# Half-array attention products in alternating pairs, in the mixing stage of a two-layer trunk

## The reference

```python
# branch A (dsa_attention), per query block of 128 tokens, 8 heads of 64, latents of 128
q_lat = jnp.einsum('bshd,rhd->bshr', q, w_uk)                       # Q
dots = jax.nn.relu(jnp.einsum('bqhd,bkd->bqhk', iq_b, ik) * idx_scale)
score = jnp.einsum('bqh,bqhk->bqk', iw_b * w_scale, dots)           # index scores
_, idx = lax.top_k(score, k_sel)                                    # 128 keys: the picks
logits = jnp.einsum('bqhr,bqkr->bqhk', ql_b, c_sel) * scale + bias  # A
p = jax.nn.softmax(logits, axis=-1)
o_lat = jnp.einsum('bqhk,bqkr->bqhr', p, c_sel)
return jnp.einsum('bqhr,rhd->bqhd', o_lat, w_uv)                    # U

# branch C (mem_attention), 4 heads of 64, 256 memory tokens
logits = jnp.einsum('bshd,bmhd->bhsm', q, k) * C_HEAD_DIM ** -0.5   # C
p = jax.nn.softmax(logits, axis=-1)
return jnp.einsum('bhsm,bmhd->bshd', p, v)                          # V
```

## Time and profile before

| what | value |
|---|---|
| median of 3 runs | 2313.9 us (2313.88 to 2318.39) |
| the profiled execution | 2316.2 us |
| its span, first to last instruction | 2314.4 us |
| mean granted TensorE clock | 0.996 |
| PE products; PE weight loads | 2259.5; 1837.9 us busy |
| DVE; ACT; POOL | 1250.9; 560.4; 1407.6 us busy |
| HBM | 90 GB/s over the span |

### The profile page before, as it was taken

One profiled execution on the slowest core, in us unless ns is written; L12 is line 12 of the kernel. 1 busy time (PEld: TensorE's weight loads), 2 busy tenths in 40 slices (PEclk: granted clock), 3 DMA queues, 4 the chain that ended last, 5 costly groups with the idle time before them and its releaser, 6 DMA issues.

```text
span 2314.4 us, 31805 instructions
## 1 busy us (share of the span) xinstructions
PE 2259.5 (98%) x10328; PEld 1837.9 (79%) x10328; DVE 1250.9 (54%) x1756; ACT 560.4 (24%) x1038; POOL 1407.6 (61%) x868
## 2 busy tenths in 40 slices
PE   7999999999999999999999999999999999999997
PEld 5888887777877788888888888877777878888885
DVE  5551554578766655145355335637787566540554
ACT  3120111443454211001121111214444532110111
POOL 4766768534445667667667666774444466666664
PEclk9999999999999999999999999999999999999998
DMA  6243223211212222322323332232112132223222
GB/s 166 93 136 104 98 79 121 83 55 55 69 60 81 93 91 91 100 100 86 105 92 126 107 105 96 80 115 73 56 60 69 46 100 91 100 82 109 99 78 77
DMA packets 67523, 209.79 MB, mean 91 GB/s; under 512 B 7369, under 2 KB 10601, under 8 KB 67177
## 3 DMA queue, kind: packets, MB, share of 16 engines
q1 hardware_dynamic: 63600, 202.84, 27.0%
q10 hardware_dynamic: 3832, 5.77, 1.1%
HBM read 204.91 MB, written 3.67 MB: 90 GB/s over the span
## 4 chain that ended last, share of the span: by engine, by line
PE 90%; DVE 7%; issue 1%; ACT 1%; DMA 0%; DVEq 0%; ACTq 0%
PE bank L521 28%; PE bank L523 27%; PE bank L522 27%; PE obank L741 1%; PE sbank L693 1%; PE tbank L714 1%; DVE u1L L1434 1%; DVE picks L1234 1%; DVE picks L1257 1%; DVE tb L1448 1%; PE sbank L688 1%; PE obank L728 1%; DVE top L1232 1%; PE sbank L675 1%; PE sbank L698 1%
## 5 line engine op out<-in xcount | busy, mean ns | idle before, releaser
L475 POOL TENSOR_TENSOR wL<-raw,wH 128x1024 fp32r<-128x1024 f32 (+3 forms) x432 | 952.6, 2205 | 36.1
L472 POOL TENSOR_SCALAR wH<-raw 128x1024 fp32r<-128x1024 f32 (+3 forms) x432 | 455.1, 1053 | 847.6 <-PE bank L523 832.5
L521 PE MATMUL bank<-u0H,wH 128*128 128x512 f32 x1408 | 552.7, 393 | 8.2 <-POOL wL L475 4.3
L523 PE MATMUL bank<-u0L,wH 128*128 128x512 f32 x1408 | 549.8, 390 | 0.0
L522 PE MATMUL bank<-u0H,wL 128*128 128x512 f32 x1408 | 549.7, 390 | 0.0
L521 PEld LDWEIGHTS bank<-u0H,wH 128*128 128x128 f32 x1408 | 265.2, 188 | 68.2 <-issue 9.0
L522 PEld LDWEIGHTS bank<-u0H,wL 128*128 128x128 f32 x1408 | 265.5, 189 | 55.5 <-issue 1.0
L523 PEld LDWEIGHTS bank<-u0L,wH 128*128 128x128 f32 x1408 | 265.4, 189 | 55.5
L521 PE MATMUL bank<-u1H,wH 128*128 128x512 f32 x704 | 295.6, 420 | 7.3 <-DVE u1L L1434 3.0
L521 PE MATMUL bank<-hidH,wH 128*128 128x512 f32 x704 | 275.1, 391 | 0.8 <-DVE hidL L1137 0.8
L523 PE MATMUL bank<-u1L,wH 128*128 128x512 f32 x704 | 275.1, 391 | 0.0
(11 more groups left out here) (175 smaller groups left out, 2400.1 us busy)
## 6 DMA issues: line engine op xcount, KB each, us to landing
raw<-in_wA SPq DMA_DIRECT2D x176, 512.0 KB, 3.3
raw<-in_wM SPq DMA_DIRECT2D x96, 512.0 KB, 3.3
raw<-in_wB SPq DMA_DIRECT2D x64, 384.0 KB, 3.0
raw<-in_wB SPq DMA_DIRECT2D x64, 320.0 KB, 2.9
raw<-in_wR SPq DMA_DIRECT2D x32, 256.0 KB, 2.6
h<-in_xT ACTq DMA_DIRECT2D x4, 512.0 KB, 7.0
mem<-in_memT SPq DMA_DIRECT2D x2, 1024.0 KB, 7.3
near_bias<-bias_rows ACTq DMA_DIRECT2D x2, 1024.0 KB, 6.8
```

The source lines that it names most:

```text
L472: pool.tensor_scalar(wH[:, w, 0:cols], raw[:, slot, 0:cols], 1.0, 0.0, ALU.mult, ALU.add).then_inc(rounded, 1)
L475: pool.tensor_tensor(wL[:, w, 0:cols], raw[:, slot, 0:cols], wH[:, w, 0:cols].bitcast(F32), ALU.subtract).then_inc(split_done, 1)
L521: pe.matmul(dst, a, hi[:, k, :], start=first and i == 0, stop=False)
L523: mm = pe.matmul(dst, a, lo[:, k, :], start=False, stop=last and i == len(tiles) - 1)
```

## The change

`attention_steps` has one Q step per block and one U step per block where there were two each, so eight steps fewer, in a new order. Each of these steps makes both halves. The C steps keep their number, but the logits of both halves are issued in the step of the first half, and the values of both in the later step, three behind the second half. Within a step the two halves alternate product by product: rows 0-63 and 64-127 for C and Q, each into a small bank of its own, columns 0-63 and 64-127 for V and U, into the two partition halves of one bank. PE waits for both small banks ahead of a C or Q pair. `olat` is two buffers. ACT copies two query halves in a Q step, and U's high and low part are one instruction each of 128 partitions. The numbers of products do not change.

C now stands at tile 0 of slots 6 to 13, scores beside tiles 6 and 7 of even slots and 1, 3, 5, 7 of odd ones, and "bc" slots 0 to 2 have no step. The last U stands behind tile 4 of slot 34, before slot 35.

```diff
 def attention_steps():
-    s = [("C", qb, hp) for qb in range(QB) for hp in range(2)]
-    s[4:4] = [("Q", 0, 0), ("Q", 0, 1)]
+    s = [("C", qb, hp) for qb in range(QB) for hp in range(2)] + [("Q", 0, 0)]
...
         if late:
-            a.insert(2, late)
-        at = a.index(("A", qb, 3))
+            a.insert(3, late)
         if qb + 1 < QB:
-            a.insert(at + 1, ("Q", qb + 1, 0))
-            a.append(("Q", qb + 1, 1))
-        at = a.index(("A", qb, 3))
-        a.insert(at + 4, ("U", qb, 0))
-        late = ("U", qb, 1)
+            a.append(("Q", qb + 1, 0))
         if qb == 0:
             a += [("B", 0, 0), ("B", 1, 0)]
+        late = ("U", qb, 0)
...
-SCORE_SLOTS = range(6, 12)
-FIRST_STEPS = 6
-ALONE = (6, 7, 8, 9, 11)
+FIRST_STEPS, FIRST_TWO = 6, 14
 AFTER = 8
-SCORES_BESIDE_TWO, SCORES_BESIDE_ONE = (1, 2, 6, 7), (2, 5, 6, 7)
+SCORES_BESIDE = ((6, 7), (1, 3, 5, 7))
+STEPLESS = (0, 1, 2)
...
+def picks_at(slot):
+    kind, i = slot
+    if kind == "bc":
+        return (0, int(i >= 3))
+    if i < 9:
+        return (0, 0)
+    if i < FIRST_TWO:
+        return (0, 2)
+    return (1, 2) if 16 <= i < 23 else (1, 1)
...
# PE, logits(i)
+                    if kind in "CQ":
+                        n, free = s_bank_free(("step", i + 1, 0) if kind == "C" else ("step", i, 1))
+                        if free:
+                            pe.wait_ge(*free)
+                        dst = [dst, sbank[n]]
                     if kind == "C":
...
-                        rows = slice(64 * b, 64 * b + 64)
                         for j in range(2):
-                            mm = pe.matmul(dst[:, j * M:(j + 1) * M], qc[rows, j, a * P:(a + 1) * P],
-                                           kc[rows, j, :], start=True, stop=True)
+                            for g in range(2):
+                                rows = slice(64 * g, 64 * g + 64)
+                                mm = pe.matmul(dst[g][:, j * M:(j + 1) * M], qc[rows, j, a * P:(a + 1) * P],
+                                               kc[rows, j, :], start=True, stop=True)
+                                if j == 1:
+                                    mm.then_inc(s_full, 1)
+                        return
...
                     elif kind == "U":
-                        pe.wait_ge(olat_ready, l * 8 + (2 * a + b + 1))
+                        pe.wait_ge(olat_ready, l * 8 + (2 * a + 2))
                         for j in range(4):
-                            hd = head(4 * b + j)
-                            mm = pe.matmul(dst[64 * b:64 * b + 64, j * P:(j + 1) * P],
-                                           pr[:, W_UV + HD * hd:W_UV + HD * hd + HD],
-                                           olat[:, j * P:(j + 1) * P], start=True, stop=True)
+                            for g in range(2):
+                                hd = head(4 * g + j)
+                                mm = pe.matmul(dst[64 * g:64 * g + 64, j * P:(j + 1) * P],
+                                               pr[:, W_UV + HD * hd:W_UV + HD * hd + HD],
+                                               olat[g][:, j * P:(j + 1) * P], start=True, stop=True)
...
# PE, values(i)
-                        if m:
-                            pe.wait_ge(yc_ready, l * 8 + m)
+                        if a:
+                            pe.wait_ge(yc_ready, l * 8 + 2 * a)
                         for j in range(2):
                             for mb in range(2):
-                                mm = pe.matmul(obank[64 * b:64 * b + 64, j * P:(j + 1) * P],
-                                               vc[:, mb, (2 * j + b) * HD:(2 * j + b + 1) * HD],
-                                               pt[:, m % 2, (2 * j + mb) * P:(2 * j + mb + 1) * P],
-                                               start=mb == 0, stop=mb == 1)
+                                for g in range(2):
+                                    mm = pe.matmul(obank[64 * g:64 * g + 64, j * P:(j + 1) * P],
+                                                   vc[:, mb, (2 * j + g) * HD:(2 * j + g + 1) * HD],
+                                                   pt[:, g, (2 * j + mb) * P:(2 * j + mb + 1) * P],
+                                                   start=mb == 0, stop=mb == 1)
+                                    if j == 1 and mb == 1:
+                                        mm.then_inc(v_full, 1)
+                        return
...
# ACT, exps(i)
                     elif kind == "Q":
-                        act.wait_ge(s_full, l * len(S_USES) + (n + 1))
-                        act.activation(qlat[:, 4 * b:4 * b + 4, :].rearrange("p a t -> p (a t)"), src[:, :],
-                                       ACT.Copy, scale=HD ** -0.5).then_inc(qlat_ready, 1)
+                        for g in range(2):
+                            act.wait_ge(s_full, l * len(S_USES) + (n + g + 1))
+                            act.activation(qlat[:, 4 * g:4 * g + 4, :].rearrange("p a t -> p (a t)"),
+                                           sbank[(n + g) % 2][:, :], ACT.Copy, scale=HD ** -0.5
+                                           ).then_inc(qlat_ready, 1)
```

More of the change, by code:

```diff
@@ L123, in slot_plan @@
     plan, at, scored = {}, 0, 0
-    per_slot = N_SCORES // len(SCORE_SLOTS)
     for s in slots:
[L126 to L129, removed]
-        else:
[L131 to L144, removed]
+        kind, i = s
+        first, second = picks_at(s)
+        scores = ()
+        if kind == "bc":
+            steps = [] if i in STEPLESS else [(AFTER, second)]
+        elif i < FIRST_STEPS:
+            steps = []
+        elif i < FIRST_TWO:
+            steps = [(0, second)]
+            scores = SCORES_BESIDE[i % 2]
+        else:
+            steps = [(4, first), (AFTER, second)]
         beside = []
@@ L149, in slot_plan @@
                 at += 1
[L150 to L153, removed]
+        for tile in scores:
+            beside.append((tile, "score", scored, 0))
+            scored += 1
         plan[s] = sorted(beside)
@@ L159, with s_uses, both @@
 SLOTS, PLAN = slot_plan()
-S_USES = [(kind, n) for _slot in SLOTS for _, kind, n, _ in PLAN[_slot] if kind == "score" or STEPS[n][0] != "N"]
-S_INDEX = {u: n for n, u in enumerate(S_USES)}
+def s_uses():
+    uses = []
+    for slot in SLOTS:
+        for _, kind, n, _ in PLAN[slot]:
+            if kind == "score":
+                uses.append((kind, n, 0))
+            elif STEPS[n][0] == "C":
+                uses += [(kind, n, 0), (kind, n + 1, 0)] if STEPS[n][2] == 0 else []
+            elif STEPS[n][0] == "Q":
+                uses += [(kind, n, 0), (kind, n, 1)]
+            elif STEPS[n][0] != "N":
+                uses.append((kind, n, 0))
+    return uses
+S_USES = s_uses()
+S_INDEX = {u: n for n, u in enumerate(S_USES)}
+def both(i, at):
+    if STEPS[i][0] != "C":
+        return [i]
+    if STEPS[i][2] != at:
+        return []
+    return [i - at, i - at + 1]
 def head(n):
@@ L269, in trunk @@
         zb = gate_bc
-        olat = relu[:, 0, :]
+        olat = [relu[:, b, :] for b in range(2)]
         pt = sg
@@ L636, in s_bank_free @@
                         return n % 2, ()
-                    kind, i = S_USES[n - 2]
+                    kind, i, part_ = S_USES[n - 2]
                     if kind == "score":
@@ L653, in score @@
                         pe.wait_ge(iq_low, l * 8 + 8)
-                    n, free = s_bank_free(("score", s))
+                    n, free = s_bank_free(("score", s, 0))
                     if free:
@@ L663, in logits @@
                     kind, a, b = STEPS[i]
-                    if kind == "N":
+                    if kind == "N" or kind == "C" and b:
                         return
-                    n, free = s_bank_free(("step", i))
+                    n, free = s_bank_free(("step", i, 0))
                     if kind != "B" and free:
@@ L683, in logits @@
                     elif kind == "Q":
[L684 removed]
+                        if a == 0:
                             pe.wait_ge(evacuated, chunk_at(l, C_IN + 9))
[L686 removed]
                         for j in range(4):
[L688 to L689 removed]
+                            for g in range(2):
+                                rows = slice(64 * g, 64 * g + 64)
+                                mm = pe.matmul(dst[g][:, j * P:(j + 1) * P], pr[rows, W_UK + P * j:W_UK + P * (j + 1)],
+                                               q[rows, j, a * P:(a + 1) * P], start=True, stop=True)
+                                if j == 3:
+                                    mm.then_inc(s_full, 1)
+                        return
                     elif kind == "A":
@@ L913, in exps @@
                         return
-                    n = S_INDEX[("step", i)]
+                    n = S_INDEX[("step", i, 0)]
                     src = sbank[n % 2]
@@ L992, in step @@
                     if i >= 3 and i - 3 in SOFTMAX:
-                        take_values(i - 3)
```

(18 more changed lines are left out.)

25 lines of the change are left out of this document (13 added, 12 removed).

## The result

| | before | the change |
|---|---|---|
| median | 2315.82 us of 4 runs (2313.88 to 2318.39) | 2292.94 us of 4 runs (2290.65 to 2294.21) |
| the profiled execution; its span | 2316.2; 2314.4 us | 2290.65; 2288.8 us |

The ratio is 0.9896, with a 95% interval of 0.9884 to 0.9907. The change is faster, as forecast, but by 23 us where 45 were forecast, and 2 us outside the range. A fourth run of before has moved its median from the 2313.9 of the forecast to 2315.8.

The account below looks back on a forecast made before the run. PE was taken as the bound, busy 98% of the span. From the profiled 2316.2 us: -38.1 for pairing, -10 for scores, +3 added gives 2271.1, stated as 2269 because that execution was 2.3 above the median; range 2260 to 2291.

Parts of the forecast that it names:

- What bounds the kernel now: Whole kernel and mixing stage: PE bounds, busy 98% of the span; DVE is nearest behind, 36.83 of 50 us.
- Price of a half step and what pairing does: C, Q, V, U steps: a half step costs 1.10 to 1.25 us; pairing saves 38.1 us, at least 10.7.
- Row B: Pool product of two 64x64 halves on different rows and columns, starting 0.01 us apart; taken as evidence for full pairing.
- The new layout of scores: Index scores in the mixing stage, set further apart in odd slots: nearly all PE waiting there goes, saving 10 us.
- What is added: Mixing stage: new PE waits for banks, copies, later picks and late probabilities cost +3 us, between -2 and +8.
- rival 2: Mixing stage: DVE delivers probabilities and slot 13 scores late, ten to twelve stalls of 1 us: 2280, chance 0.10.
- Rivals 1, 3 and 4: In order: only one axis pairs, 2283, chance 0.12; nothing pairs, 2296, 0.06; each change of half drains the array, 2329, 0.04.
- The range: Whole kernel: 2260 with no new stall, to 2291 with DVE stalls and one axis unpaired, together in part.

Follow-up runs that it names:

- serial: The change with all products of one half issued before the other's in each C, Q, V and U step, instead of in turn: 2302.87 us, ratio 0.9931.
- psum_both: The change with the score relu and the first sum of A-step logits written in place in PSUM: 2274.36 us, ratio 0.9812.
- psum_late: psum_both with the two rounds of picks of slot 13 moved to slots 14 and 15: 2271.19 us, ratio 0.9796.

## Why the prediction was right in sign and wrong in size

- **What bounds the kernel now**: right for before, but not what bounds it after. I judged DVE by one stretch of 50 us, at 36.83. In 520 to 540 it was at 17.13 of 20 already, with PE never waiting. The change takes some 18 us of PE's time per layer (35.5 / 2) away from beside it, and that time was the cover.
- **Price of a half step and what pairing does**, 38.1 us: right. The four kinds reach what follows in 1.02 to 1.09 us, and 35.5 us came out between the two kernels without picks, 37 if their remaining waits are taken out (35.5 + 3.1 - 1.3, an estimate). Row B carried over to halves that share rows or columns. The rule of the Trainium skill that spoke against V and U (TensorE: Matmul & The Clock Gate, Part 3) would have left them about the 1.89 us worked out for serial; sixteen records with the same rows in 1.02 and 1.03 us speak against it.
- **The new layout of scores**, 10 us: wrong in its reason, and its size was not measured by itself. All of PE's wait at that line went, 6.0 us and 1.4 for the exponentials. But it stays gone with the old tiles. My remark that it would return at slot 13 if DVE ran 3 us late describes what psum_both showed (2.5 us there); in the change the stall came one slot earlier, at the C step, which waits for both banks. Whether it would have come with the banks awaited one by one wasn't tried.
- **What is added**, +3 us with bounds of -2 and +8: this is the step that failed. I reasoned that the pair's banks had been freed a tile before, and that the values products had waited 1.2 us in all. Both hold as long as DVE is in time. psum_late, in which it nearly is, shows what its lateness costs: 2292.94 - 2271.19 = 21.8 us. Of these 13.8 are idle (the 15.8 shown above, less the 2.0 left in psum_late), and the clock makes some 7: it fell behind two of the three stalls of a layer, and four stretches of 20 us at 0.91 instead of 1.00 are 4 x 20 x 0.09 = 7.2 (an estimate). So the term was 21.8 and not 3, which is 18.8 of the 24 us between the forecast of 2269 and the 2293 measured. The pairs brought 2.6 less, and 1.9 are the median of before that a fourth run moved. The stage is 25.6 us of span shorter in two layers, 11.6 in layer one and 14.1 in layer two from the norm ahead of it to the one behind it, and not 23 in each.
- **The rivals**: rival 2 is what happened, DVE delivering late in slot 13's neighbourhood and in query blocks 1 and 2. I put it at 2280, with ten to twelve stalls of 1 us; six long ones came, of 2 to 2.4 us, each with a total cost of up to 3.6 (21.8 / 6). My reason against it, that a fifth of DVE is free, took a mean for a reserve. Rivals 1, 3 and 4 are excluded by the rows of pairs above; serial shows that an order in which rival 1 or 3 would have been partly true exists.
- **The range**: its high end of 2291 came from rivals priced too low. With rival 2 at its measured 22 us instead of 11 it would have held the result.

What I could have read and didn't: beside the row with 899 ns in the earlier trace rows, the same addition over 384 columns stood at 1237 ns in the mean. An operation that takes longer on fewer columns is waiting for something, and nothing in the program holds it once it has started. The row of before:

```profile
L1257 DVE SCALAR_TENSOR_TENSOR picks<-relu,iw,picks 128x384 f32<-128x384 f32 x7 | 8.7, 1237 | 0.8 <-DVE picks L1234 0.2
```

## What to carry to other kernels

Where a busy engine is relieved, list the next engine's load in short stretches, and the longest single duration of each of its operations, before the saving is counted; a mean over 50 us says nothing about 2.4 us. Half-array products that alternate between two halves cost one half's time here, even when they share rows or columns; issued half after half, eight records each, they gave up half of that gain, and only four records each kept it. And where GpSimd reads SBUF beside VectorE, an addition with one operand left in PSUM was never stopped here (0.42 us in 18 of 18 cases): one such edit was worth 18.8 us behind the change, half of what the pairs themselves are worth, and with the edit of the scores 7.8 us in the kernel before, where DVE had time over.

## What the hardware showed that was not expected

- Halves that share rows (V, U) or columns (C, Q) run side by side as fully as B's, which share neither: 16 records of V, U and Q in 1.02 to 1.09 us, 8 of C in 1.06.
- With all of one half first, products of the other half started when three records were left ahead of them (serial, 707.80 against 708.12), and U takes 1.51 us for 1.03.
- Behind a stall of 2 to 2.4 us PE's clock can fall to its lower level, 1.2 GHz: 0.43 us between big products for 0.23, and a granted 0.91 over those 20 us. Behind the stall of 2.19 at 530.05 it did not: 0.32 us from 530.68 to 531.00, and 1.00 granted. It is not the length of the stall or the work around it: in layer two the same stall of 2.19 was followed by the lower level, and that of 2.02 was not. What tells them apart stays open.
- An addition of 128 columns on DVE took 2.06 us beside a subtraction on POOL and 0.29 without it, and 0.29 beside one again once an operand lay in PSUM (psum_both).
